# Attention softmax on one core: the weights divided by their sum inside the transposing product, in place of an elementwise scaling and a plain transpose

## The reference

```python
logits = jnp.where(key_pos[None, :] <= t_pos[:, None], logits, -jnp.inf)
p = jax.nn.softmax(logits, axis=-1).astype(v.dtype)
return jnp.einsum('bhqk,bhkd->bhqd', p, v)
```

## Time and profile before

| | us |
|---|---|
| median of 3 runs | 3016.28 |
| lowest, highest | 3016.21, 3024.34 |
| the profiled execution | 3016.28 |
| its span in the trace | 3014.4 |
| TensorE busy in the span | 2650.9 (88%) |
| VectorE busy | 1540.1 (51%) |
| ScalarE busy | 1272.7 (42%) |
| DMA, mean | 130 GB/s |

### The profile page before, as it was taken

One profiled execution on the slowest core, in us unless ns is written; L12 is line 12 of the kernel. 1 busy time (PEld: TensorE's weight loads), 2 busy tenths in 40 slices (PEclk: granted clock), 3 DMA queues, 4 the chain that ended last, 5 costly groups with the idle time before them and its releaser, 6 DMA issues. The chain is left out here.

```text
span 3014.4 us, 31719 instructions
## 1 busy us (share of the span) xinstructions
PE 2650.9 (88%) x11144; PEld 1806.7 (60%) x11144; DVE 1540.1 (51%) x2279; ACT 1272.7 (42%) x1941; POOL 268.8 (9%) x196
## 2 busy tenths in 40 slices
PE   6899887889999889789996899968978999699897
PEld 2564465467777557467774555535756777555554
DVE  6215077332223346643455777745554345577775
ACT  6302244432222353533233677725354333277673
POOL 0000000000000010000001243301000000023330
PEclk9889998999999899999997999989999999799998
DMA  9311100032212212022123999951201222289994
GB/s 346 132 46 39 56 5 1 29 111 84 70 56 97 75 56 101 11 84 84 56 93 114 326 320 317 313 197 56 84 29 56 84 84 72 88 287 321 322 323 177
DMA packets 263292, 392.29 MB, mean 130 GB/s; under 512 B 23663, under 2 KB 185471, under 8 KB 263167
## 3 DMA queue, kind: packets, MB, share of 16 engines
q1 hardware_dynamic: 236448, 340.55, 33.8%
q10 hardware_dynamic: 14367, 33.34, 2.9%
q0 software_dynamic: 12352, 16.81, 1.8%
HBM read 386.44 MB, written 29.36 MB: 138 GB/s over the span
## 5 line engine op out<-in xcount | busy, mean ns | idle before, releaser
L186 PE MATMUL banks<-arena_parts,hT_parts 128*128 128x512 f32 x1056 | 423.5, 401 | 37.7 <-DVE ring_parts L216 26.2
L187 PE MATMUL banks<-ring_parts,arena_parts 128*80 128x512 f32 (+1 forms) x1136 | 453.9, 400 | 0.0
L188 PE MATMUL banks<-arena_parts,ring_parts 128*128 128x512 f32 x1056 | 418.9, 397 | 0.0
L216 DVE TENSOR_TENSOR ring_parts<-ring,hT_parts 128x1024 fp32r<-128x1024 f32 x148 | 181.3, 1225 | 391.2 <-ACT hT_parts L212 388.5
L2856 DVE TENSOR_TENSOR ring_parts<-ring,hT_parts 128x2048 fp32r<-128x2048 f32 x128 | 292.6, 2287 | 161.6 <-ACT hT_parts L2750 158.1
L186 PE MATMUL banks<-hT_parts,arena_parts 128*80 128x512 f32 (+1 forms) x824 | 337.4, 409 | 40.6 <-DVE hT_parts L2853 23.6
L212 ACT ACTIVATE hT_parts<-ring 128x1024 fp32r<-128x1024 f32 x148 | 156.6, 1058 | 452.8 <-PE banks L188 452.0
L187 PE MATMUL banks<-hT_parts 128*128 128x512 f32 x864 | 344.1, 398 | 0.0
L2750 ACT ACTIVATE hT_parts<-ring 128x2048 fp32r<-128x2048 f32 x128 | 244.4, 1911 | 213.8 <-DMA ring<-in_w_exp_up 161.0
L162 PE MATMUL banks<-ring,hT 128*128 128x512 f32 (+3 forms) x672 | 261.8, 547 | 15.0 <-POOLq L155 6.8
L186 PEld LDWEIGHTS banks<-arena_parts,hT_parts 128*128 128x128 f32 x1056 | 200.5, 190 | 97.9 <-issue 48.3
(11 more groups left out here) (465 smaller groups left out, 3871.9 us busy)
## 6 DMA issues: line engine op xcount, KB each, us to landing
ring<-in_w_exp_gate SPq DMA_DIRECT2D x64, 1024.0 KB, 5.8
ring<-in_w_exp_up SPq DMA_DIRECT2D x64, 1024.0 KB, 8.9
ring<-in_w_exp_down SPq DMA_DIRECT2D x128, 512.0 KB
ring<-in_w_in SPq DMA_DIRECT2D x58, 1024.0 KB, 7.0
ring<-in_w_mod SPq DMA_DIRECT2D x24, 1024.0 KB, 14.2
ring<-in_w_gate SPq DMA_DIRECT2D x11, 1024.0 KB, 7.8
ring<-in_w_up SPq DMA_DIRECT2D x11, 1024.0 KB, 9.7
ring<-in_w_down SPq DMA_DIRECT2D x22, 512.0 KB, 4.0
```

The costliest lines, as they stand in the source:

```text
L186: nc.tensor.matmul(out, lh, rh, start=start and i == 0, stop=False)
L187: nc.tensor.matmul(out, lh, rl, start=False, stop=False)
L188: last = nc.tensor.matmul(out, ll, rh, start=False, stop=stop and i == len(terms) - 1)
L216: nc.vector.tensor_tensor(unit_of(ring_r, n, q), unit_of(ring, n, q), hi_unit(s[1]).bitcast(F32), ALU.subtract).then_inc(S("unit_lo"), 1)
```

## The change

A new tile `sum_diag` of 2 x 128 columns lies in the shared memory at column 18576, where a stage that is over by then had a scratch tile. VectorE no longer scales the row of `p`. It multiplies the 128x128 identity by the reciprocal of the sum of each row, which gives a diagonal matrix, for two units in turn. TensorE multiplies each block of the unscaled `p`, as stationary operand, with this diagonal as moving operand, in a matmul in place of the transpose. VectorE waits in addition, from u = 3 on, for the transposing products of unit u - 3, which read the same half of `sum_diag`.

```diff
         UNITS = H2 * LT
+        sum_diag = A(18576, 2, P)
...
                 for j in range(i + 1):
-                    last = nc.tensor.transpose(ps[:, 2 + n % 2, j * P:(j + 1) * P], p[:, n % 2, j * P:(j + 1) * P], ident[:, :])
+                    last = nc.tensor.matmul(ps[:, 2 + n % 2, j * P:(j + 1) * P], p[:, n % 2, j * P:(j + 1) * P], sum_diag[:, n % 2, :], start=True, stop=True)
...
                 if u:
-                    w, c = ((u - 1) % LT + 1) * P, 1 - c
+                    c = 1 - c
                     dve.wait_ge(S(nm + "_exp"), u)
+                    if u >= 3:
+                        dve.wait_ge(S(nm + "_tr"), u - 2)
                     V.reciprocal(stat[:, 6 + c:7 + c], stat[:, 2 + c:3 + c])
                     dve.drain()
-                    V.tensor_scalar(p[:, c, 0:w], p[:, c, 0:w], stat[:, 6 + c:7 + c], None, ALU.mult).then_inc(S(nm + "_pn"), 1)
+                    V.tensor_scalar(sum_diag[:, c, :], ident[:, :], stat[:, 6 + c:7 + c], None, ALU.mult).then_inc(S(nm + "_pn"), 1)
```

## The result

The kernel after takes 3039.25 us in the median of six runs (3025.62 to 3044.76), beside 3016.24 us of the kernel before (3013.78 to 3024.34): a ratio of 1.0067, between 1.0043 and 1.0091. It is slower, as forecast, but the range ended at 3035. The profiled execution is the shortest of the six, 3025.62 us with a span of 3023.9. It lies near the forecast of 3027.5, the median does not, and the nearness is luck: in this profile the four stages that the change touches take 15.4 us more than in the profile before, and the rest of the program 6.0 us less.

The account below looks back on a forecast made before the run. TensorE (PE), busy for 88% of the span, was taken as the bound. Two layers of fox at 3.7 and mla at 1.9 us add 11.2 us to 3016.28: forecast 3027.5 us (chance 0.60), range 3019 to 3035.

Parts of the forecast that it names:

- The surcharge: On PE, each of 160 blocks takes two passes in place of one transpose: 0.103 us more a block.
- the absent surcharge: Rival: on PE the second pass hides behind the weight load; 3014.3 us, not slower; chance 0.12.
- four passes' worth: Rival: on PE a block costs four times 0.117 us, 0.47 us; 3059 us in all; chance 0.03.
- Fox has no slack: Answers the rival that fox takes up the surcharge as mla does: 7.6 us more, 3023.9 us; chance 0.17.
- third rival: New products' weight loads in fox and mla do not run ahead: 9 us more, 3037 us; chance 0.08.
- Fox: 4.4 us a stage in place of 3.7: In fox, 30 blocks on PE's chain add 3.1 us and the last seven 0.64: 3.7 us a stage.
- The stop at the scaling: In fox's first head, PE's 0.6 us wait for VectorE takes up the 0.31 us of the three early blocks.
- Mla: 2.8 us a stage in place of 1.9: In mla, first head 0.39 us, two later heads 0.37 each, tail 0.77: 1.9 us a stage.
- The replay: One head of mla worked through from values to values, with PE's waits for VectorE: 0.37 us more a head.
- The shorter scaling: On VectorE, all 64 scalings take the 128-column form: 6.4 us less, counting only where PE waits for it.
- The clock: the step that failed: At fox and mla starts: clock already full, shifts gain or lose a microsecond each; 3 us to either side, outside the sum.
- the 0.85 behind mla: PE's average granted clock behind mla, where it starts the next stage after idling at a clock not yet full.

Follow-up runs that it names:

- second comparison: The kernel after, unedited, run again against new runs of the kernel before: median 3030.7 us of eleven runs, ratio 1.0045.
- VectorE's order: The kernel before, with VectorE scaling a head's last unit ahead of the next maximum from u = 8 on: 3014.69 us, ratio 0.9999.
- long pause: TensorE waits for eight ScalarE copies ahead of each fox stage, in both kernels: 3046.27 us on the kernel before, 3064.85 on the kernel after.
- fp32r kernel: The kernel after with p and the diagonal stored in rounded 32-bit format, one pass in place of two: 3027.32 us, ratio 1.0033.

## Why the prediction was right and wrong

**Right in sign and in mechanism.** The surcharge is the second pass; both cleaner experiments say so, one with the pass and without the diagonal (+15.5 us in the four stages), the other with the diagonal and without the pass (mla -0.4 us a stage). In fox it lies on PE's chain, in mla it goes through a chain with slack. Of the rivals, the absent surcharge falls with the first timeline; so do four passes' worth. Fox has no slack: a head grows by 1.21 us. PE never waits for a new weight load: the loads themselves start late for no visible reason 7 times in mla of layer 1, 3.1 us in all, where the transposes' did 8 times, 4.9 us, and once in fox, 0.4 us; so the third rival falls too.

**The block was mis-sized by a tenth to a quarter.** The step was "the surcharge is d = 0.220 - 0.117 = 0.103 us". In a long run it is (4.57 - 3.77)/7 = 0.114 us, a tenth more, from the third head's values to the last in mla (1101.29 - 1096.72 = 4.57 after, 1101.85 - 1098.08 = 3.77 before). In the short units ten blocks of a fox head add 1.21 us, so 0.121 each, and in the mla head above the four runs add 0.36 + 0.51 + 0.14 + 0.28 = 1.29 us, 0.129 each. The price of a pass is 0.112 us rather than the 0.110 taken from L162, and the unevenness at a change of line, which the prediction gave to the transposes alone, is paid by the new products too.

**Fox: 4.4 us a stage in place of 3.7.** Its shape was right. The first head grows by 1.30 us, the next two by 1.21 each and the tail by 0.66, where the prediction had 1.03 three times and 0.64. The stop at the scaling in the first head took up the early blocks, as forecast: it goes from 0.58 us to this (timeline of PE, kernel after)

```profile
1272.90 0.91 PE L1772 MATMUL banks<-arena 128*128 128x128 f32 x6 [0.24 <-DVE arena L1820]
```

and that product starts 1272.90 - 1265.21 = 7.69 us after the first logits, where it was 1272.76 - 1265.12 = 7.64.

**Mla: 2.8 us a stage in place of 1.9.** The first head grows by 0.80 (forecast 0.39), the next two by 0.60 (0.37), the tail by 0.80 (0.77). The replay had each wait right: unit 7's products start 3.79 us after the values, forecast 3.75, and the 0.49 us stop is gone. From there on the larger block counts in full. The eight passes take 0.97 in place of the replay's 0.88, scores(11) is 0.45 late where 0.27 was forecast, and unit 9's products 0.32 where 0.16 was. A chain with slack passes on what exceeds the slack, so an error of a quarter in the block (0.129 for 0.103) became one of two thirds in the head (0.60 for 0.37).

These two together are 14.4 in place of 11.2 us, 3030.7 us by the prediction's own sum. The second comparison bears it out as far as it can: by its ratio the change costs 8.8 to 18.4 us, the runs included that lost the clock.

**VectorE.** The new wait for the products costs nothing that any view shows. The shorter scaling is worth 1.1 us in all, read from the kernel that has the product without it.

**The clock: the step that failed.** The prediction said that at 1.00 "there is no slower level from which a denser PE could climb", and gave "each of the four starts" a microsecond either way. It looked up and not down. A fox stage that loses the clock costs 10.5 us in the kernel after and 8.5 in the kernel before, not 1. Its price came from the 0.85 behind mla. That row is the next stage beginning at the lower level, after PE had been idle for 4.24 us, and costs about a microsecond. It says nothing of the four starts to which the prediction applied it: in the profile before, all four stages of the change run at 1.00 from their first logits on, and had all of that to lose. Of the 11.8 us between the forecast and the median, 3.2 are the block and 8.6 are left for this step. Counted by the mean clock, 7 of the 17 runs of the kernel after in the first two comparisons have 0.946 or less, and 8 of the 67 of the kernel before over the four groups of experiments. The first comparison had three such runs of six and two more at 0.947, and its median stands those 8.6 us above the 14.4. That these runs lost a fox stage is inferred from their clock and from the profile of the second comparison; the only profile of the first is of the one run at 0.951. The inference has a limit: the 3035.27 us at 0.949 is as long without a low clock, and VectorE's order had 0.946 with both fox stages whole.

Shown is: where the time goes (fox at 0.50), that in the one profile of the kernel after that has it, it starts ahead of the stage's new products, that the kernel before can be brought to it by a start delayed by half a microsecond (one stage of two) or by 5.6 (both), that transposes are no protection, and that the same half microsecond takes the clock of both fox stages in the profile of the kernel after, and by the clock in all four of its runs, but of one stage in the profile of the kernel before. In how many of that kernel's other runs it did, the clock does not tell for certain. What stays open is why the kernel after is nearer to the fall. Nothing between its mla and its fox is changed, and its fox starts behind the same 0.71 us of idle time. That its 2.8 us in mla move the start against the points at which the clock is decided is argued, not shown, and the shift is not simply 2.8 us: from the first logits of mla to those of fox it is 194.2 in place of 190.8 us in layer 1, where fox kept the clock, and only 192.5 in place of 191.8 in the layer 2 that lost it. Only two profiles of the kernel after at its own order exist.

## What to carry to other kernels

- A transpose of 32-bit data by the plain product costs a second pass per block, 0.12 us here. Folding a row scaling into it is worth that only where the scaling is on the path; here VectorE had 6.4 us to give and 1.1 of it was wanted.
- Ask of each stage not only whether a higher clock could be reached, but what the lower one would cost, and how long it would stay. Here the median of the first comparison stood 8.6 us above what the longer stages explain, and the lost clock of one fox stage costs 10.6.
- When runs of one kernel fall into two groups, put them beside their mean clock before explaining the median, and profile one of each group.

## What was not expected of the chip

- In fox the lower level stayed for 20 to 31 us in all profiles that lost it at its start, while PE was busy with hardly a stop (22.00 of 22 us in the stretch above); in mla of layer 2 of the kernel after it stayed for 3.4 us. Both falls came at a like point, 2.9 and 2.7 us after the first logits.
- Without the long pause, five of the six falls in fox came 2.4 to 2.9 us after its first logits; the sixth, in the fp32r kernel's fox of layer 1, came 10.0 us in and stayed for 10.2. With the long pause all four came 2.3 to 2.6 us ahead of them. Mla of layer 2 lost the clock in 5 of the 14 profiles, of both kernels, 2.5 to 2.7 us after its first logits, for 3.4 or 6.8 us, and took 1.0 to 2.1 us longer; mla of layer 1 never did.
- Two 32-bit passes with weights of 128 columns follow at 0.112 us a pass, a transpose's single pass at 0.110 to 0.113 and one of fp32r at 0.113 ((0.61 - 0.27)/3). The weight load, 0.19 us (median) for the first and the last, 0.14 for a transpose, lies beside them.
- One mean clock, 0.945 or 0.946, stood for different things: a fox stage at the lower level in one kernel, longer stages elsewhere in another (VectorE's order). The clock of a run says that something was lost, and only a profile says where.
